# A two-layer mixer and expert trunk on one core: one y buffer with a combine for each unit, and the shared expert, LayerNorm and routing put in another order

## What is computed

```python
scores = sigmoid(xt @ router_w)
top_e = top_k(masked(scores + router_bias), 8)          # 64 experts, group-limited
gate = scores[top_e] / sum(scores[top_e]) * 2.5
routed = sum over the 8 of  gate * ((silu(h @ w_gate[e]) * (h @ w_up[e])) @ w_down[e])
shared = (silu(xt @ sh_gate) * (xt @ sh_up)) @ sh_down
x = layer_norm(alpha * x + routed + shared)
```

## Time and profile before

| | |
|---|---|
| median of 3 runs | 1344.94 us (1344.16 to 1346.04) |
| profiled execution: its own time, its span | 1344.52 us, 1342.8 us |
| busy: PE, DVE, ACT | 1227.3 us (91%), 516.6 us (38%), 322.4 us (24%) |
| DMA queue of SP | 463.50 MB |
| chain that ended last | PE 59%, DMA 33% (`ring<-in_w_up` 32%) |
| TensorE's mean granted clock | 0.965 of full speed |

### The profile page before, as it was taken

One profiled execution on the slowest core, in us unless ns is written; L12 is line 12 of the kernel. 1 busy time (PEld: TensorE's weight loads), 2 busy tenths in 40 slices (PEclk: granted clock), 3 DMA queues, 4 the chain that ended last, 5 costly groups with the idle time before them and its releaser, 6 DMA issues.

```text
span 1342.8 us, 19213 instructions
## 1 busy us (share of the span) xinstructions
PE 1227.3 (91%) x7592; PEld 737.2 (55%) x7592; DVE 516.6 (38%) x1096; ACT 322.4 (24%) x539; POOL 9.3 (1%) x29
## 2 busy tenths in 40 slices
PE   8999999988888988899999999999998888888998
PEld 8986444444344443348999997644543434344443
DVE  5656333222222222236476666622321222222213
ACT  4442112111111111214544443211111111111110
POOL 0000000000000000000000000000000000000000
PEclk9999999988889989999999999999999888999989
DMA  9956889999999999989544436589999999999993
GB/s 331 393 200 255 332 331 423 420 421 421 421 421 420 422 421 421 420 321 399 188 172 177 163 122 254 208 346 390 421 421 421 420 421 421 420 421 422 421 420 132
DMA packets 83992, 469.10 MB, mean 349 GB/s; under 512 B 7209, under 2 KB 19625, under 8 KB 34875
## 3 DMA queue, kind: packets, MB, share of 16 engines
q1 hardware_dynamic: 82448, 463.50, 85.0%
q10 hardware_dynamic: 1451, 4.33, 0.8%
HBM read 466.76 MB, written 1.05 MB: 348 GB/s over the span
## 4 chain that ended last, share of the span: by engine, by line
PE 59%; DMA 33%; SPq 3%; DVE 3%; issue 2%; ACT 0%; POOL 0%; POOLq 0%; DVEq 0%; ACTq 0%
DMA ring<-in_w_up 32%; PE ps L699 21%; PE ps L591 10%; PE ps L603 6%; PE ps L626 5%; PE ps L723 5%; PE ps L679 3%; PE ps L761 2%; PE ps L737 2%; SPq L409 2%; SPq L429 1%; PE ps L770 1%; PE ps L578 1%; PE ps L667 1%; PE ps L876 1%
## 5 line engine op out<-in xcount | busy, mean ns | idle before, releaser
L699 PE MATMUL ps<-ring,xsT 128*32 128x512 f32 (+1 forms) x2432 | 398.0, 647 | 94.1 <-DMA ring<-in_w_up 94.0
L699 PEld LDWEIGHTS ps<-ring,xsT 128*32 128x32 f32 (+1 forms) x2432 | 126.7, 128 | 359.2 <-issue 358.9
L723 PE MATMUL ps<-ring,hidT 128*32 128x512 f32 (+1 forms) x1216 | 189.7, 596 | 1.0 <-ACT hidT L1032 1.0
L1333 DVE SCALAR_TENSOR_TENSOR sig<-sig,slot_gate,ps 128x256 f32<-128x256 f32 x52 | 25.0, 480 | 424.2 <-ACT sig L1028 424.2
L1158 DVE TENSOR_TENSOR ring_low<-ring,wh 128x1024 fp32r<-128x1024 f32 (+1 forms) x112 | 129.2, 1156 | 103.5 <-ACT wh L972 102.8
L972 ACT CAST wh<-ring 128x1024 fp32r<-128x1024 f32 (+1 forms) x112 | 110.6, 989 | 166.8 <-PE ps L591 69.0
L1028 ACT ACTIVATE sig<-ps 128x256 f32<-128x256 f32 x52 | 20.0, 384 | 477.3 <-PE ps L699 477.3
L1347 DVE TENSOR_TENSOR yl<-ps,yh 128x512 fp32r<-128x512 f32 x104 | 72.0, 692 | 131.3 <-ACT yh L1037 131.3
L591 PE MATMUL ps<-xTh,wh 128*128 128x256 f32 x384 | 109.5, 285 | 3.6 <-DVE ring_low L1158 3.6
L723 PEld LDWEIGHTS ps<-ring,hidT 128*32 128x32 f32 (+1 forms) x1216 | 52.2, 119 | 105.4 <-issue 103.6
L591 PE MATMUL ps<-xTh,ring_low 128*128 128x256 f32 x384 | 109.5, 285 | 0.0
(11 more groups left out here) (202 smaller groups left out, 1263.5 us busy)
## 6 DMA issues: line engine op xcount, KB each, us to landing
ring<-in_w_down SPq DMA_DIRECT2D x128, 1024.0 KB, 25.7
ring<-in_w_gate SPq DMA_DIRECT2D x124, 1024.0 KB, 22.1
ring<-in_w_up SPq DMA_DIRECT2D x124, 1024.0 KB, 25.2
ring<-in_b_w_in SPq DMA_DIRECT2D x8, 3072.0 KB, 16.1
ring<-in_a_w_in SPq DMA_DIRECT2D x12, 1024.0 KB, 12.2
ring<-in_b_w_out SPq DMA_DIRECT2D x4, 3072.0 KB, 10.3
ring<-in_w_gate SPq DMA_DIRECT2D x8, 512.0 KB, 6.4
ring<-in_w_up SPq DMA_DIRECT2D x8, 512.0 KB, 8.4
```

Source lines behind the costliest of these rows:

```text
L699: last = nc.tensor.matmul(ps[first:first + width, p, :], xsT[:, c, p * P + first:p * P + first + width], slot_gu(slot_of(layer, k))[:, c], ...
L723: last = nc.tensor.matmul(ps[first:first + width, 4 + h, :], hidT[:, p, kk * P + first:kk * P + first + width], slot_dn(slot_of(layer, k)) ...
```

## The change

- There is one `yh` and one `yl`. `combine(u)` handles one unit with two matmuls for each n: unit 2r - 1 after the gate and up of unit 2r, unit 2r after the gate and up of unit 2r + 1. `turn` then stands behind the whole combine. There are as many combine matmuls as before and twice as many adds on DVE.
- The shared expert's down product stands in `combine(4)` and accumulates in the same banks. The residual `ALPHA * X` is done by the adds of `combine(0)`.
- PE's order in the first round, the first LayerNorm in halves and tile by tile, the routing products and DVE's sorting steps are moved; 12 matmuls that only kept PE busy (`keep_clock_up(4, 12)`) go.
- `spread_row` uses a high and a low part in fp32r, made once in layer 0's mixer.
- In the last round unit 24 is finished and combined ahead of unit 25's gate and up. SP's last refills come in the same unit order as the others.
- The same arithmetic is done in all of it.

```diff
@@ -483,12 +484,9 @@
                 load_gate_up(layer, KNOWN - 1, KNOWN - 1)
                 refill(layer, 0, "down")
                 refill(layer, 1, "down")
-                for u in range(2, 2 * ROUNDS - 4):
+                for u in range(2, 2 * ROUNDS):
                     refill(layer, u, "gate_up")
                     refill(layer, u, "down")
-                for part in ("gate_up", "down"):
-                    for u in (2 * ROUNDS - 4, 2 * ROUNDS - 3):
-                        refill(layer, u, part)
                 sp.wait_ge(W.over, W.past.over + 1)
@@ -575,8 +573,9 @@
             def spread_row(r, bank):
                 for h in range(2):
-                    last = nc.tensor.matmul(ps[:, bank + h, :], ident[0:18, 2 * r + h:2 * r + h + 1].to_broadcast([18, P]),
-                                            row[:], start=True, stop=True)
+                    own = ident_r[:, 2 * r + h:2 * r + h + 1].to_broadcast([18, P])
+                    for part in (row_high, row_low):
+                        last = nc.tensor.matmul(ps[:, bank + h, :], own, part[:], start=(part is row_high), stop=(part is row_low))
                 return last
@@ -642,10 +641,13 @@
                             for t in range(TT):
-                                output(n - 1, t)
-                                last = output(n, t)
-                                last.then_inc(W.out_done, 1)
-                                spread_row(4 * layer + t, 2 * t).then_inc(W.ln_rows, 1)
+                                for h in range(2):
+                                    output(n - 1, t, (h,))
+                                    output(n, t, (h,)).then_inc(W.out_done, 1)
+                                if t == 0:
+                                    pe.wait_ge(g.row_low, 1)
+                                    spread_row(4 * layer, 0).then_inc(W.ln_rows, 1)
+                                    spread_row(4 * layer + 1, 2).then_inc(W.ln_rows, 1)
                             break
                     last.then_inc(W.used, 1)
@@ -726,22 +728,22 @@
                                                     start=(kk == 0), stop=(kk == HC - 1))
                     last.then_inc(W.y_done, 1)
-            def combine(W, r, parts):
-                for n in parts:
+            def combine(W, u, shared=None):
+                r, p = u // 2, u % 2
+                pe.wait_ge(W.yl_ready, W.past.yl_ready + 2 * (u + 1))
+                pe.wait_ge(W.c_ready, W.past.c_ready + r + 1)
+                for n in range(4):
                     t, h = n // 2, n % 2
-                    if 4 * r + n >= 2:
-                        pe.wait_ge(W.comb_taken, W.past.comb_taken + 4 * r + n - 1)
-                    for p in range(2):
-                        for part in (yh, yl):
-                            last = nc.tensor.matmul(ps[:, 2 + n % 2, :], back[:, p, t * P:(t + 1) * P],
-                                                    part[p][:, h * HALF:(h + 1) * HALF],
-                                                    start=(p == 0 and part is yh), stop=(p == 1 and part is yl))
+                    if u > 1 or n >= 2:
+                        pe.wait_ge(W.comb_taken, W.past.comb_taken + 4 * u + n - 1)
+                    dst = ps[:, (2 if u else 6) + h, :]
+                    for part in (yh, yl):
+                        last = nc.tensor.matmul(dst, back[:, p, t * P:(t + 1) * P], part[:, h * HALF:(h + 1) * HALF],
+                                                start=(part is yh), stop=(part is yl and shared is None))
+                    if shared is not None:
+                        last = shared(t, h, dst)
                     last.then_inc(W.comb_done, 1)
-            def combine_ready(W, r):
-                pe.wait_ge(W.yl_ready, W.past.yl_ready + 4 * (r + 1))
-                pe.wait_ge(W.c_ready, W.past.c_ready + r + 1)
             def experts(layer):
...
                     turn(W, r, 0)
-                    combine(W, r - 1, (2, 3))
                     down(layer, r, 0)
+                    if r == 1:
+                        pe.wait_ge(W.comb_taken, W.past.comb_taken + 8)
+                        for t in range(TT):
+                            for kk in range(HC):
+                                last = nc.tensor.transpose(ps[:, 3, kk * T + t * P:kk * T + (t + 1) * P], shid[:, t, kk:H:HC], ident[:])
+                        last.then_inc(W.sh_hT, 1)
                     gate_up(layer, r, 1)
+                    if r == 1:
+                        pe.wait_ge(W.sh_hT_ready, W.past.sh_hT_ready + 1)
+                        pe.wait_ge(g.sh_dn, 16 * (layer + 1))
+                    combine(W, 2 * r, shared_down if r == 2 else None)
                     pe.wait_ge(W.s_ready, W.past.s_ready + r + 2)
                     gather(W, r + 1, (0, 1))
@@ -865,29 +864,28 @@
                 pe.wait_ge(W.info_taken, W.past.info_taken + ROUNDS)
                 spread_row(4 * layer + 2, 6).then_inc(W.gain_out, 1)
                 gate_up(layer, r, 0)
-                combine_ready(W, r - 1)
-                combine(W, r - 1, (0, 1))
+                combine(W, 2 * r - 1)
                 turn(W, r, 0)
-                combine(W, r - 1, (2, 3))
+                down(layer, r, 0)
                 pe.wait_ge(W.gain_ready, W.past.gain_ready + 1)
-                for n in range(4):
-                    t, h = n // 2, n % 2
-                    pe.wait_ge(W.comb_taken, W.past.comb_taken + 4 * r)
-                    nc.tensor.matmul(ps[:, SUM_BANKS[t] + h, :], ident[:], X[:, t, h * HALF:(h + 1) * HALF], start=True, stop=False)
-                gate_up(layer, r, 1)
-                down(layer, r, 0)
-                turn(W, r, 1)
-                down(layer, r, 1)
+                pe.wait_ge(W.comb_taken, W.past.comb_taken + 8 * r)
+                for t in range(TT):
+                    for h in range(2):
+                        nc.tensor.matmul(ps[:, SUM_BANKS[t] + h, :], ident[:], X[:, t, h * HALF:(h + 1) * HALF], start=True, stop=False)
                 pe.wait_ge(W.c_ready, W.past.c_ready + ROUNDS)
                 for p in range(2):
-                    for n in range(4):
-                        t, h = n // 2, n % 2
+                    if p:
+                        gate_up(layer, r, 1)
+                        turn(W, r, 1)
+                        down(layer, r, 1)
+                    for h in range(2):
                         pe.wait_ge(W.yl_ready, W.past.yl_ready + 4 * r + 2 * p + h + 1)
-                        for part in (yh, yl):
-                            last = nc.tensor.matmul(ps[:, SUM_BANKS[t] + h, :], back[:, p, t * P:(t + 1) * P],
-                                                    part[p][:, h * HALF:(h + 1) * HALF], start=False, stop=(p == 1 and part is yl))
-                        if p == 1:
-                            last.then_inc(W.comb_done, 1)
+                        for t in range(TT):
+                            for part in (yh, yl):
+                                last = nc.tensor.matmul(ps[:, SUM_BANKS[t] + h, :], back[:, p, t * P:(t + 1) * P],
+                                                        part[:, h * HALF:(h + 1) * HALF], start=False, stop=(p == 1 and part is yl))
+                            if p:
+                                last.then_inc(W.comb_done, 1)
@@ -1168,10 +1169,12 @@
                     return ps[:, bank:bank + 2, :].rearrange("p a b -> p (a b)")
                 def statistics(t):
-                    dve.wait_ge(W.out_done, t + 1)
-                    step(nc.vector.scalar_tensor_tensor(X[:, t, :], X[:, t, :], ALPHA, rows_of(4 + 2 * t), ALU.mult, ALU.add))
                     for h in range(2):
-                        last = nc.vector.bn_stats(stats[:, t, h, :], X[:, t, h * HALF:(h + 1) * HALF])
+                        dve.wait_ge(W.out_done, 2 * t + h + 1)
+                        cols = slice(h * HALF, (h + 1) * HALF)
+                        step(nc.vector.scalar_tensor_tensor(X[:, t, cols], X[:, t, cols], ALPHA, ps[:, 4 + 2 * t + h, :],
+                                                            ALU.mult, ALU.add))
+                        last = nc.vector.bn_stats(stats[:, t, h, :], X[:, t, cols])
                     step(last)
@@ -1186,12 +1189,10 @@
                     nc.vector.scalar_tensor_tensor(X[:, t, :], X[:, t, :], rstd[:, t:t + 1], rows_of(2),
                                                    ALU.mult, ALU.add).then_inc(W.x_ready, 1)
-                statistics(0)
-                centre(0)
-                statistics(1)
-                scale(0)
-                centre(1)
-                scale(1)
+                for t in range(TT):
+                    statistics(t)
+                    centre(t)
+                    scale(t)
             def sums(t):
...
+                    nc.vector.tensor_tensor(yl[:, cols], ps[:, 4 + h, :], yh[:, cols].bitcast(FP32),
                                             ALU.subtract).then_inc(W.yl_ready, 1)
```

(32 more changed lines are left out.)

221 lines of the change are left out of this document (105 added, 116 removed).

## The result

The changed kernel takes **1359.47 us** (median of 4 runs, 1357.98 to 1361.17) against 1344.55 of the kernel before beside it (4 runs): ratio 1.0113, 95% interval 1.0099 to 1.0127. It is 1.1% slower, and outside the range that was given (1340.3 to 1349.6). The profiled execution has a span of 1359.5 us for 1342.8, 16.7 more.

What follows compares the result with a forecast made beforehand. DMA loads were taken to bound the middle, PE and DVE the start, PE the end. The terms -5.2 + 7.2 - 0.95 - 1.9 + 0.6 = -0.25 gave 1344.7 us, range 1340.3 to 1349.6.

Steps and rivals of the forecast that it cites:

- Reading of the kernel: Whole layer: PE and DVE decide the start, DMA loads set the middle, PE time counts again in the end.
- The clock ... in the LayerNorm stretch ... +0.6: LayerNorm stretch without its 12 fillers: lost clock could cost 1.9 us in a layer; +0.6, bounds 0 and +3.8.
- -2.6 us in each layer: Start of each layer: loads flow back to back 2.9 us sooner, less 0.3 for a possible gap at unit 3.
- the next loads join without a gap: Start, behind expert 5's load: unit 2's gate and up done at about 177.6, loads running to 179.8.
- +3.6 us in each layer: End of each layer: +5.3 up to unit 25's down product, -1.3 behind it, 0.4 less for the last spread row.
- 6.25 for 7.54: End, behind the last down product: y's low part, half a combine and one half's statistics take 6.25 us, -1.3.
- -1.9: Ends of the layers: one of two enters at full clock, saving 1.9 us; bounds 0 and -3.8.
- -0.95: Layer 1's mixer, where PE is busy throughout: the spread row takes 0.95 us instead of 1.9.
- The clock falls: Rival, chance 0.19: LayerNorm stretch drops to 1.2 GHz in both layers and both ends enter slow, +4.85, 1349.8 us.
- No gain at the start: Rival, chance 0.02: expert 5's late load eats the whole gain of the start, +4.95, 1349.9 us.

Runs made afterwards that it cites:

- e1_fill: Changed kernel with filler matmuls put back into TensorE's waits of the LayerNorm stretch, 6 behind the first router product and 3 behind the second transposes: 1352.89 us.
- e2_sh_first: Changed kernel with all eight pieces of the second shared gate and up product ahead of the first combine: 1353.20 us.
- e3_down0: Changed kernel with only SP's queue changed, the down loads of unit 0's slots issued ahead of the wait for expert 5's load: 1359.42 us.
- e9_end_clock: Changed kernel with fillers in the end: 12 ahead of unit 23's gate and up, 6 behind unit 25's, 10 behind its down product: 1355.22 us.
- e11_before_clock: Kernel before the change with only 18 fillers added in the wait ahead of unit 23's gate and up: 1344.45 us.
- e10_all_clock: Changed kernel with LayerNorm fillers, shared product first, new last-round order, turns and gathers inside combines, and fillers ahead of unit 23's and 25's gate and up: 1338.34 us.

## Why the prediction was wrong, point by point

- **Reading of the kernel, right.** The middle is the DMA engines'; combines of 3.3 us, turn to down product and the longer rounds cost nothing there; the idle stretch of 7 us ahead of expert 5 came as forecast.
- **"The clock ... in the LayerNorm stretch ... +0.6": the step that failed most.** Mis-sized: against e1_fill it is 4.3 us in layer 0 (27.0 for 22.7) and 3.8 in layer 1 (26.5 for 22.7), 8.1 in all, and e1_fill's time is 6.6 less. The prediction bounded it by 3.8 for both layers, one slow product of 1.9 in each. But the granted clock stays at 0.50 for the second transposes (0.8 more than in e1_fill), the second router product (1.7 more) and the first 4 us of the shared product (1.9 more), one behind the other on the chain. It also took the length of a single wait (up to 1.7) as evidence that the clock would hold, by the earlier trace rows; here a stretch broken into pieces lost it with no wait over 1.38. The Trainium skill (TensorE: Matmul & The Clock Gate, "A second HAM failure mode: psum-queue depth-cycling") tells of a bf16 kernel that cycled through PSUM banks and idled so often for short times that its clock swung between half and full. The prediction named this and set it aside for the rounds. The LayerNorm stretch is another kind of work, small fp32 products, but the trace agrees that short idle times can do it: a granted clock of 0.50 from 112 to 122 us. In the rounds, where the combines' waits are as short, it does not (0.98 from 189 to 548 us).
- **"-2.6 us in each layer" for the start.** Without the clock the LayerNorm part is right to 0.2 us. combine(0), for which the 2.4 stands without a row, took 3.0 (155.82 to 158.79), and the shared product's end came when forecast even so, 25.9 us behind the start of unit 1's gate and up for 25.65. The rest failed in "the next loads join without a gap": unit 2's releases came 2.3 us later behind the first half loads than forecast (184.0 - 138.54 = 45.5 for 177.6 - 134.4 = 43.2): 1.7 of it is its product at half clock (8.7 for 7.05), which the prediction did not count, 0.4 expert 5's load, which took that much longer from the shared product's end to unit 2's start (7.5 for 7.1). The gap in the loads cost some 2 us in each layer (+2.4 and +2.2 for +0.4). e2_sh_first and e3_down0 show that it is this chain.
- **"+3.6 us in each layer" for the end.** Found: 5.4 and 4.8. The order itself is right: from unit 23 to unit 25's down product 50.9 and 52.1 for 51.7. Behind it, "6.25 for 7.54" was wrong. In layer 1 it is 6.9: in DVE's order both halves' statistics stand behind the second half's low part (done at 1347.42), they ran in one piece (1.29 at 1348.03), and the half that was to lie under the combine did not. In layer 0 it is 8.5, 1.7 of it by the down product at half clock.
- **"-1.9" for one end at full clock.** No end had it: unit 23's product was slow behind 2.41 us of wait as behind 3.32. The price of 1.9 holds for the changed kernel (in e9_end_clock unit 22 to unit 24 is 1.3 and 3.1 us shorter, where unit 23's product is 1.7 and 2.9 faster), but not for the kernel before, from which the prediction took it: there e11_before_clock finds it hidden by a load.
- **"-0.95" for the spread row.** Four matmuls do stand where 1.9 us stood (1312.67 - 1311.55 = 1.1), but layer 1's mixer starts at half clock for longer (granted clock 0.50 and 0.85 in the first two stretches of 4 us, from 622 to 630, where it was 0.67 and 0.90 from 612 to 620), and its length is 223.4 us for 223.2.
- **The rivals.** "The clock falls" had the right mechanism and place, but allowed 3.8 us for both LayerNorm stretches, where e1_fill shows 8.1, and knew nothing of unit 2 or the last down product. "No gain at the start" was right in its sign and in part in its reason: expert 5's late load cost 2 us a layer, but the LayerNorm stretch, which was to bring 3.2, lost 1.0 and 0.5 by the clock.

That a late shared product opens the gap, that the fillers carry the clock, and that the last round lacked cover is shown by runs. That the longer half-clock stretch ate the 1.1 us in layer 1's mixer is argued from the trace and was not tried; nor was a version with SyncE's old order of the last loads, which might shorten unit 25's wait in e10_all_clock.

## What to carry to other kernels

Where TensorE's products are the critical chain, filler matmuls that look useless may be what keeps that chain at full clock: when an edit removes them or cuts the work around them in pieces, price every product behind it at double length until the clock comes back, not one. When a load is late, follow it to the end: who waits for it, what that one releases, and whether the queue has run dry by then; filling an idle stretch with other ready loads only moves it. And before a slow product is priced, look whether a load would be waited for in its place.

## What the runs showed of the hardware that was not expected

- Gate and up products behind a wait of 2.41 us (551.82, changed kernel) ran at half clock, 8.77; behind 2.13 they ran fast in the kernel before but slow in e11_before_clock (995.05, 8.78 after 2.12). The same TensorE program saw both at nearly the same length: unit 2 took 8.78 after a wait of 3.32 us in the changed kernel and 7.09 after 3.22 in e3_down0, and the last down product 5.34 and 3.64 in the changed kernel's two layers, behind waits of 1.5 and 0.46 us in both. So the length of the last wait alone does not tell whether the clock falls.
- 24 matmul instructions of 128x128 in each layer, 2.9 us of work without a result, carried 10.6 us of a 1345 us kernel.
